# A hybrid decoder step on one core: the front's work in another order, and the first recurrent pair's fills copied out before its exponentials

## The reference, cut to what matters

```python
p = rmsnorm(x, norm_mix_g) @ w_in
a_q, a_k, a_v, i_q, i_k, i_w, p_b, c_q, gates = split_last(p, IN_SIZES)
# a_q, a_k, i_q, i_k are rotated (rope_partial)
...
def index_topk(iq, iw, ik, q_pos, topk):
    s = jax.nn.relu(jnp.einsum('bqhd,bld->bqhl', iq, ik))
    score = jnp.einsum('bqhl,bqh->bql', s, iw).astype(jnp.float32)
    ...
    _, idx = lax.top_k(score, topk)
...
# prompt: blocks of 128 queries, topk = 128, keys of the prompt
# sample: topk = 256, keys of the cached pages (cache_idx_k[page_table]) and the new ones
...
ps = p_b + (prev - p_b) * mu
r, k, v, wl, al, gl = split_last(ps, RWKV_SIZES)
w_log = -jax.nn.softplus(-(w0 + jnp.tanh(wl) @ w_up)) - 0.5
decay = jnp.exp(-jnp.exp(w_log.astype(jnp.float32)))
...
mk, mv = jnp.split(rmsnorm(mem, norm_mem_g) @ w_mem_kv, 2, axis=-1)
```

## Time and profile before

| | us |
|---|---|
| median of three runs | 1349.66 |
| lowest and highest | 1349.17, 1350.88 |
| profiled execution | 1349.81 |
| its span | 1347.9 |
| TensorE busy in the span | 1234.8 (92%) |
| VectorE busy | 710.7 (53%) |
| ScalarE busy | 407.2 (30%) |
| GpSimd busy | 86.3 (6%) |

### The profile page before, as it was taken

One profiled execution on the slowest core, in us unless ns is written; L12 is line 12 of the kernel. 1 busy time (PEld: TensorE's weight loads), 2 busy tenths in 40 slices (PEclk: granted clock), 3 DMA queues, 4 the chain that ended last, 5 costly groups with the idle time before them and its releaser, 6 DMA issues.

```text
span 1347.9 us, 25134 instructions
## 1 busy us (share of the span) xinstructions
PE 1234.8 (92%) x10585; PEld 1094.1 (81%) x10589; DVE 710.7 (53%) x1126; ACT 407.2 (30%) x791; POOL 86.3 (6%) x140
## 2 busy tenths in 40 slices
PE   6699699889969988998998999999999999999995
PEld 4476476658657777887887889999999999999994
DVE  5499798714043284365346337755544434434445
ACT  2110144424322423343234234233333123123120
POOL 0100100002102042002001002000000000000000
PEclk9899799999989999999999999999999999999997
DMA  7113143513500022022013215562122312223211
GB/s 305 31 28 156 35 167 120 178 35 156 200 0 10 33 79 89 18 97 97 18 56 118 73 43 161 170 235 95 63 94 74 114 63 95 95 67 121 77 50 67
DMA packets 39218, 127.52 MB, mean 95 GB/s; under 512 B 5203, under 2 KB 17491, under 8 KB 29635
## 3 DMA queue, kind: packets, MB, share of 16 engines
q1 hardware_dynamic: 37666, 121.36, 25.3%
q0 software_dynamic: 1440, 4.56, 1.0%
HBM read 111.77 MB, written 14.13 MB: 93 GB/s over the span
## 4 chain that ended last, share of the span: by engine, by line
PE 78%; DVE 15%; ACT 2%; issue 2%; DMA 1%; POOL 1%; SPq 0%; DVEq 0%; ACTq 0%; POOLq 0%
PE ps L923 13%; PE ps L924 12%; PE ps L927 12%; PE ps L951 8%; PE ps L1281 4%; PE ps L960 3%; PE ps L961 3%; PE ps L962 3%; PE ps L904 2%; DVE R L1999 2%; DVE small L1998 2%; PE ps L1233 2%; PE ps L946 1%; PE ps L949 1%; DVE wl L558 1%
## 5 line engine op out<-in xcount | busy, mean ns | idle before, releaser
L548 ACT ACTIVATE wh<-land 128x1024 fp32r<-128x1024 f32 (+1 forms) x120 | 116.2, 970 | 185.6 <-PE ps L927 185.6
L951 PE MATMUL ps<-xn,ring 128*128 128x272 f32 x576 | 149.4, 403 | 9.4 <-ACT pb L1593 9.4
L558 DVE TENSOR_TENSOR wl<-land,wh 128x1024 fp32r<-128x1024 f32 (+1 forms) x120 | 136.0, 1136 | 27.7 <-ACT wh L548 26.9
L923 PE MATMUL ps<-xhi,wh 128*128 128x272 f32 x512 | 138.9, 289 | 2.3 <-DVE wl L558 1.2
L923 PE MATMUL ps<-hh,wh 128*128 128x272 f32 x512 | 138.8, 288 | 0.0
L924 PE MATMUL ps<-hl,wh 128*128 128x272 f32 x512 | 138.3, 288 | 0.0
L924 PE MATMUL ps<-xlo,wh 128*128 128x272 f32 x512 | 138.3, 288 | 0.0
L951 PEld LDWEIGHTS ps<-xn,ring 128*128 128x128 f32 x576 | 105.4, 192 | 34.6 <-ACT pb L1593 9.8
L960 PE MATMUL ps<-xhi,wh 128*128 128x272 f32 x384 | 124.2, 324 | 4.2 <-issue 3.6
L961 PE MATMUL ps<-xlo,wh 128*128 128x272 f32 x384 | 113.3, 295 | 0.0
L962 PE MATMUL ps<-xhi,wl 128*128 128x272 f32 x384 | 113.2, 295 | 0.0
(11 more groups left out here) (407 smaller groups left out, 2368.8 us busy)
## 6 DMA issues: line engine op xcount, KB each, us to landing
land<-in_slabs SPq DMA_DIRECT2D x48, 1024.0 KB, 4.8
ring<-in_slabs SPq DMA_DIRECT2D x17, 1024.0 KB, 8.1
gates<-R SPq DMA_DIRECT2D x24, 272.0 KB, 2.0
merge<-gates SPq DMA_DIRECT2D x24, 272.0 KB, 4.1
land<-in_slabs SPq DMA_DIRECT2D x12, 512.0 KB, 3.9
xT<-in_mks SPq DMA_DIRECT2D x8, 512.0 KB, 4.9
R<-in_kv SPq DMA_DIRECT2D x24, 128.0 KB, 2.0
pb<-in_kv SPq DMA_DIRECT2D x24, 128.0 KB, 2.0
```

The costliest lines, as they stand in the source:

```text
L548: act.activation(hi, src, ACT.Copy).then_inc(s["weights_hi"], 1)
L558: eng.tensor_tensor(lo, src, hi.bitcast(F32), ALU.subtract).then_inc(s["weights_lo"], 1)
L923: pe.matmul(ps[:, b + h, 0:HALF], whi[:, k], hi[k][:, c], start=a, stop=False)
L951: mm = pe.matmul(ps[:, b, 0:HALF], W[:, k, c0_:c0_ + w], xn3[:, k, cols], start=a, stop=z)
```

## The change

*Loads.* SyncE loads the norm vectors first, then two of eight blocks of x, slab 0, the other blocks of x, the matrix of ones, slab 1 and the rest. The head weights in slab 0 are padded from 4 to 32 columns a block. One row of cached keys (`kv_row(0)`) is issued later.

*Front, TensorE.* The head weights become 32-column products on four column groups, summed by a product with `sel` where transposes stood. Rotations and prompt scores are laid between the blocks of the products. The page product stands behind job 6, and behind it stand the memory's norm, the sums over heads, jobs 7 to 9 with the rotations 5 to 7, the transposes of av, and 24 fill steps under a new name, `("pre", 0)`.

*Front, the others.* VectorE does the blocks t = 1 and t = 2, with the rotations 3 and 4 and the copies into `zi` after t = 1, then waits for the page product, does the memory's norm and the copy into `ss`, and then block t = 3, with the rotations 5 and 6 inside and 7 behind. ScalarE keeps block 3's relu in a space of its own (`rl3`).

*Plan.* 24 steps go to `("pre", 0)`, and places of the loop from u = 13 on get 3 where they got 4. In the first pair `("scan", 0)`, a new place, gets 24, `("prep", 0, 1)` 10 where it had 14, `("prep", 0, 2)` none where it had 8, and the 12 that closed the pair are gone. ScalarE's copies of `("scan", 0)` stand ahead of the exponentials. The sums agree at the end of the loop (160 steps) and at the first `tm` (272).

```diff
@@ fill_plan
-    waits = [(("p", u), 5 if u < 13 else 4) for u in range(36)]
+    waits = [(("pre", 0), 24)]
+    waits += [(("p", u), 5 if u < 13 else 3) for u in range(36)]
...
-        waits += [(("prep", j, n), b) for n, b in enumerate((8, 8, 8) if j else (8, 14, 8))]
+        if j == 0:
+            waits += [(("prep", 0, 0), 8), (("scan", 0), 24), (("prep", 0, 1), 10), (("prep", 0, 2), 0)]
+        else:
+            waits += [(("prep", j, n), 8) for n in range(3)]
@@ SyncE
+            x_pair(0)
...
-            stream(0, 2)
+            stream(0, 1)
+            for n in range(1, 4):
+                x_pair(n)
+            sp.dma_start(cst[:, 0:first], i["const"][:, 0:first]).then_inc(s["ones_in"], 16)
+            stream(1, 2)
@@ TensorE, front
+            part(4, xn3, 0, 2)
+            prompt_scores(2)
+            part(4, xn3, 2, 5)
+            prompt_scores(3)
+            part(4, xn3, 5, KT)
+            part(5, xn3, 0, 5)
+            pe.wait_ge(s["relu"], 12)
+            rope(3)
+            part(5, xn3, 5, KT)
+            part(6, xn3, 0, 2)
+            rope(4)
+            part(6, xn3, 2, KT)
+
+            pe.wait_ge(s["padded"], 5)
+            pe.wait_ge(s["rope_sin"], 5)
             for q in range(2):
                 pe.wait_ge(s[f"ki_in{q}"], 128 * 4)
-            pe.wait_ge(s["relu"], 12)
             for b in range(DB):
...
+            norm(1, NMEM)
             pe.wait_ge(s["selected"], 1)
...
+            part(7, xn3, 0, KT)
...
+            pe.wait_ge(s["norm_out"], 16)
+            fill("pre", 0)
@@ TensorE and ScalarE, first pair
+                    fill("scan", 0)
...
+                    evacs("scan", 0)
@@ VectorE
+            for t in range(1, 3):
+                row_scores(t)
                 for _ in range(TOPK_P // 8):
-                    take_eight(sc, m8)
...
             dve.wait_ge(s["ki_used"], 8)
             dve.tensor_scalar(rs, flat, 0.0, iws, ALU.max, ALU.mult).then_inc(s["selected"], 1)
+            norm(1, memT, memn, NMEM, "norm_mem_g")
             dve.wait_ge(s["i_rows"], 2)
...
+            row_scores(3)
+            for n in range(TOPK_P // 8):
+                if n in (6, 10):
+                    rope(5 if n == 6 else 6)
+                take_eight(scp, m8)
+            row_bias(3)
+            rope(7)
```

More of the change, by code:

```diff
@@ L612, in _, with x_pair @@
             first = COFF["cos"][0]
[L613 to L616, removed]
+            sp.dma_start(vec[:, :], i["vec"]).then_inc(s["vec_in"], 16)
+            def x_pair(n):
+                sp.dma_start(xT3[:, 2 * n:2 * n + 2], i["xT"][:, 2 * n:2 * n + 2]).then_inc(s[f"x_in{n}"], 16)
+            x_pair(0)
             def stream(first, last):
@@ L992, in _, with part, prompt_scores @@
                 job(0, xg3, only=k)
-            pe.wait_ge(s["ones_in"], 32)
+            pe.wait_ge(s["ones_in"], 16)
             norm_sum(0)
[L995 to L1011, removed]
+            slab_wait(pe, JOBS[1][2])
+            W, b = slab(0), bank_of(1)
+            for h in range(2):
+                for k in range(KT):
+                    g = slice(32 * (k % 4), 32 * (k % 4) + 32)
+                    mm = pe.matmul(ps[g, b + h, 0:HALF], W[:, k, P:P + 32], xg3[:, k, h * HALF:(h + 1) * HALF],
+                                   start=(k < 4), stop=(k >= 4))
+            mm.then_inc(s["gemm_done"], 1)
+            def part(n, src, first, last):
+                for k in range(first, last):
+                    job(n, src, only=k)
+            def prompt_scores(t):
                 for h in range(4):
@@ L1017, in _ @@
                               start=True, stop=True).then_inc(s["iscore"], 1)
[L1018 to L1022, removed]
+            job(2, xg3)
+            part(3, xg3, 0, 3)
+            pe.wait_ge(s["inputs_in"], 16)
+            out_of(1, pe)
+            for t in range(5):
+                w = P if t < 4 else NS
+                mm = pe.matmul(ps[0:w, 7, 4 * t:4 * t + 4], iwT[:, P * t:P * t + w], k_("sel")[:, 0:4], start=True, stop=True)
+            mm.then_inc(s["i_rows"], 1)
+            rope(0)
+            part(3, xg3, 3, 6)
+            pe.wait_ge(s["padded"], 1)
+            rope(1)
+            part(3, xg3, 6, KT)
+            rope(2)
+            pe.wait_ge(s["rope_out"], 3)
+            prompt_scores(1)
+            part(4, xn3, 0, 2)
[12 more added lines that the diff above has]
+            pe.wait_ge(s["rope_sin"], 5)
             for q in range(2):
                 pe.wait_ge(s[f"ki_in{q}"], 128 * 4)
-            pe.wait_ge(s["relu"], 12)
             for b in range(DB):
@@ L1036, in _ @@
             mm.then_inc(s["i_rows"], 1)
[L1037 to L1041, removed]
+            part(7, xn3, 0, KT)
+            pe.wait_ge(s["selected"], 2)
+            pe.wait_ge(s["norm_rt"], 2)
+            rope(5)
+            part(8, xn3, 0, 2)
+            rope(6)
+            part(8, xn3, 2, KT)
+            part(9, xn3, 0, 2)
+            rope(7)
+            part(9, xn3, 2, KT)
             out_of(job_at("av"), pe)
@@ L1098, in _ @@
                 if v == 1:
-                    pe.wait_ge(s["ss_out"], 1)
+                    pe.wait_ge(s["selected"], 2)
                 fill("p", 2 * v)
@@ L1197, in _ @@
             fill("need", "pb", 8)
-            pe.wait_ge(s["za_set"], 3)
+            pe.wait_ge(s["padded"], 8)
             pe.wait_ge(s["x_exp"], 16)
@@ L1531, in square @@
                     act.wait_ge(s["norm_ss"], KT * n + k - 1)
-                if n == 0 and k % 4 == 0:
-                    act.wait_ge(s[f"x_in{k // 4}"], 16)
+                if n == 0 and k % 2 == 0:
+                    act.wait_ge(s[f"x_in{k // 2}"], 16)
                 if n == 2:
@@ L1617, in _ @@
             act.wait_ge(s["pool_step"], 2)
+            act.activation(small[:, 142:143], epsc, ACT.Square)
             norm(0, xT3, TOK)
-            act.wait_ge(s["aux_in"], 48)
-            norm(1, memT, NMEM)
-            act.wait_ge(s["norm_out"], 16)
+            act.wait_ge(s["norm_out"], 8)
             for t in range(1, 4):
@@ L1989, in _ @@
                 else:
-                    ins.then_inc(s["zi_set"], 1)
-            dve.wait_ge(s["zi_set"], 5)
+                    ins.then_inc(s["padded"], 1)
+            dve.tensor_copy(biasp[:, 0, 0:P], k_("caus")).then_inc(s["tables"], 1)
+            rope(0)
+            rope(1)
+            take(3, iq[:, 1])
+            rope(2)
+            dve.wait_ge(s["padded"], 1)
             flat = ps[:, 4:7].rearrange("p a b -> p (a b)")[:, 0:KEYS]
-            dve.tensor_copy(biasp[:, 0, 0:P], k_("caus")).then_inc(s["bias_done"], 1)
             def take_eight(sc, m8):
@@ L2001, in _, with row_scores @@
             m8 = small[:, 132:140]
-            for t in range(1, 4):
+            def row_scores(t):
                 n = P * (t + 1)
-                sc = scp[:, 0:n]
+                sc, rows = scp[:, 0:n], rl if t < 3 else rl3
                 for h in range(4):
```

112 lines of the change are left out of this document (58 added, 54 removed).

## The result

The changed kernel takes 1356.07 us (median of five, 1355.03 to 1356.88); the kernel before, timed beside it, 1349.17 (1346.04 to 1350.88). The ratio is 1.0053, with a 95% interval of 1.0038 to 1.0069: slower by half a per cent, where 1340.5 was forecast. The profiled execution has a span of 1353.2 us against 1347.9.

A forecast was written before the change was run, and what follows sets the result against it. TensorE was taken to carry the kernel, with a chain over three engines ending the front. Front +7.5, loop -6.4 and first pair -10.3 gave -9.2 us: 1349.7 to 1340.5, range 1334 to 1347.

The forecast's parts named there:

- Ahead of the page product: Front: TensorE arrives earlier, the pages don't; edits cost nothing, new wait of 17 to 30 us until about 101.7.
- Behind the page product: Front: serial chain from page product through norm, third block and rotations; loop starts at 164.3 instead of 156.79, +7.5 us.
- the term for the page product: Front: 15.70 us at full clock plus 2.2 lost after the gap, 17.9 in all, ending at 119.6.
- The rest of the chain: Front, after the product: reciprocal 129.7, scores copied 131.1, third block to 159.2, score at 164.3; TensorE's queue to 164.4.
- the product stays at half clock: Rival, front: page product takes 31.4 us instead of 17.9, +13.5, kernel 1354.0; chance 0.05.
- The loop: Prompt loop: 24 fill steps fewer, of which 13 count at 0.48 plus 0.15; -6.4 us, loop 120.2.
- The first pair: First recurrent pair: copies no longer behind the exponentials, transposes at about 389.7 instead of 399.99; -10.3 us.

The follow-up runs named there:

- e7: Changed kernel with VectorE's third block ahead of its wait for the page product, rotations 5 to 7 behind: 1355.48 us, ratio 1.0049.
- e12: Changed kernel without the front's 24 fill steps, the loop's budgets as before: 1362.74 us, ratio 1.0102.
- e4: Changed kernel with an unread product over the other 64 rows beside each of the page product's 16 wide passes: 1339.18 us, ratio 0.9917.
- e3: Changed kernel with 7 unread 128-row products between the wait for the pages and the page product: 1344.97 us, ratio 0.9965.
- e10: e8 with 16 of the front's 24 fill steps also ahead of the page product and VectorE's norm inside its second block: 1319.49 us, ratio 0.9762.
- e8: Changed kernel with jobs 7 to 9 and the norm in TensorE's wait, and the third block ahead of VectorE's wait: 1327.09 us, ratio 0.9836.
- e1: Kernel before with only the first pair's new plan and copies: 1338.35 us, ratio 0.9922.
- e5: Changed kernel with 60 unread products in TensorE's wait for the pages: five of ten executions 1340.2 to 1340.8 us, four 1352.7 to 1356.8.
- e9: e8 with unread products over the other 64 rows beside the page product's passes: 1326.38 us, ratio 0.9815.
- e6: Changed kernel with jobs 7, 8, 9 and the memory's norm in TensorE's wait, ahead of the page product: 1349.53 us, ratio 0.9989.
- e2: Changed kernel with 52 unread products in TensorE's wait for the pages: 1354.38 us, ratio 1.0024.

## Why the prediction was wrong

**Ahead of the page product: right.** The pages and nothing else bring it on. The wait was 26.32 us (17 to 30 forecast), the last page 1.9 us later than set, of which 1.2 is the first issue's (21.93 against 20.72).

**Behind the page product: the step that failed.** It is the term for the page product: 15.70 at full clock and 2.2 lost after the gap, which says that the clock comes back early in the product. It did not come back in it at all. The product took 30.90, 13.0 more than the 17.9; the norm behind it, still at half clock in its first part, took 1.7 more. With the pages' 1.9 this is 16.6, and the loop started 16.0 later than forecast. The rest of the chain was right within a microsecond, its order too: the third block behind the product, TensorE's queue and VectorE's ending together (e7 shows the one, e12 the other).

I had the mechanism as a rival, with its price: the product stays at half clock, 1354.0, chance 0.05; the kernel takes 1356.07. What I held against it was a wrong reading of the earlier trace rows. The prompt's scores did come back to full clock after 6.14 us of passes over 64 rows. But they are not "the same 64 rows": the code gives their heads the lower and the upper 64 in turn, so that both halves of TensorE work, while the page product uses the lower half alone. e4 fits that as the difference: with the upper half in use as well, the clock was back after some 4 us, and the time was 1339.2. That the product was slow by its clock and not by its pages, and that the clock had fallen in the wait, is shown by e3 (burst behind the wait, fast rows) and e10 (no wait, fast rows). That the idle half of the rows kept the clock down is the reading that fits e4, the prompt's scores and e8's head sums; no run changes the rows and nothing else. And the kernel before had never shown how the product fares from a standing start, since there it followed on dense work: a measured duration holds for the clock at which it was measured. The rule that I quoted, the Trainium skill's "TensorE: Matmul & The Clock Gate", section "Why this matters for your kernels", that idle gaps put TensorE back to half rate, is borne out here, by the 0.50 behind the wait.

One reading was off without touching the sum. In the kernel before it was not the page product's end alone that VectorE followed: it reads the product at 136.98 with no wait, 2.3 us behind the end at 134.64, because its own third block ended only then.

**The loop: right.** -7.2 where -6.4 was forecast. The wait behind a late first fill grew from 1.24 to 1.70, as expected:

```profile
269.68 0.63 PE L1115 MATMUL ps<-cst,R 128*128 128x128 f32 x4 [1.70 <-ACT R L1686]
```

**The first pair: right.** -9.8 in the trace and -10.5 by e1, for -10.3. The exponentials still wait for VectorE's sum, not for the copies put ahead of them:

```profile
397.53 1.28 ACT L1809 ACT_TABLE_LOAD   x1
400.53 0.66 ACT L1809 ACTIVATE R<-R 128x544 f32<-128x544 f32 x1 [1.72 <-DVE R L2223]
```

What stays open: whether e5's two groups differ in the gap that was left, as the spread of TensorE's arrival between e8 and e9 suggests, or in what the same gap does. Only an execution with a gap was profiled.

## What to carry to other kernels

When a change makes TensorE wait, ask what it does right after the wait, and price that work at 1.2 GHz to its end unless a row shows the same work, on the same rows of the array, coming back from a standing start. Fill such a wait with the kernel's own later work up to its end, not almost to it: behind gaps of 4.18 and 4.14 us (the profiled e6 and e8) the product stayed slow, and with none it ran at full clock (e10). Where two engines' queues of equal length hang on one wait, moving work out of one of them gains nothing (e7); it has to be both (e8).

## What was not expected of the hardware

The page product's passes over 64 of 128 rows ran for 30.9 us at a granted clock of 0.50 without a break between them, and for 15.7 at 1.00 when dense work led into them without a gap. Useless work made the kernel faster, twice: 5.73 us of it ahead of the product (e3), and as many passes again beside it (e4). And behind gaps of 3.02 and 1.24 us the clock fell only inside the product, within its first two samples (the profiled e2 and e5).
